# Who stores the diagonal blocks: ScalarE's queue instead of SyncE's, and a reordered first chunk

## The reference

```python
h = concatenate([meta_tokens, x])
proj = rms_norm(h) @ w_in          # q, k, v, z, two gates a and b per head, pool input, two output gates
qkv = silu(causal_depthwise_conv(qkv, 4 taps));  q, k = l2_normalize(q), l2_normalize(k)
o = chunk_gated_delta_rule(q, k, v, g, beta)       # 8 heads of 128
y = sigmoid(g_a) * (rms(o) * silu(z)) + sigmoid(g_b) * multiscale_causal_pool(pool_in)
h = h + y @ w_out
h = h + (silu(gate) * val) @ w_down                # from rms_norm(h) @ w_up, conv of 3 taps
out = rms_norm(h)[16:]

# inside chunk_gated_delta_rule, for each chunk and head:
lower = strict_lower((k * beta) @ k.T * decay)     # step KK
tinv  = inverse(lower + eye)                       # unit lower triangular
u, w  = tinv @ (v * beta), tinv @ (k * beta * exp(g))
v_new = u - w @ state;  o_i = q @ state + qk @ v_new
state = state * g_tot + k.T @ v_new                # carried from chunk to chunk
```

## Time and profile before

| what | value |
|---|---|
| median of 3 executions | 1813.52 us (1812.1 to 1817.27) |
| profiled execution | 1815.34 us, its span 1813.5 us |
| mean granted TensorE clock | 0.974 |
| TensorE busy | 1703.6 us, 94% of the span |
| VectorE, ScalarE, GpSimd busy | 899.9, 609.6, 479.9 us |
| transfers | 167.41 MB, 92 GB/s over the span |
| SyncE's queue, ScalarE's queue | 130.39 MB, 36.28 MB |

### The profile page before, as it was taken

The page is one execution under the profiler, slowest core; times in us unless marked ns, Lnnn a source line. Parts: engine busy times, 40 slices in busy tenths (PEclk is TensorE's granted clock), DMA queues, the critical chain, the costliest instruction groups (busy, mean ns, idle before and its releaser), DMA issues.

```text
span 1813.5 us, 30705 instructions
## 1 busy us (share of the span) xinstructions
PE 1703.6 (94%) x12131; PEld 1626.9 (90%) x12131; DVE 899.9 (50%) x971; ACT 609.6 (34%) x984; POOL 479.9 (26%) x469
## 2 busy tenths in 40 slices
PE   6999999975989998998969989999999999999997
PEld 6999999975989988898869989989989989989986
DVE  5565544573435444344352365455455455456457
ACT  6334474432424343343332442212212212212213
POOL 3222222152443344424402122122222222222220
PEclk9999999987999999999989999999999999999999
DMA  5223433335353635454395101111111111111112
GB/s 184 82 90 111 130 122 98 97 105 162 105 137 108 159 93 140 102 142 116 87 289 184 34 26 58 35 57 47 35 58 46 35 58 46 35 58 46 36 45 93
DMA packets 239653, 167.41 MB, mean 92 GB/s; under 512 B 43880, under 2 KB 225991, under 8 KB 238456
## 3 DMA queue, kind: packets, MB, share of 16 engines
q1 hardware_dynamic: 205492, 130.39, 25.4%
q10 hardware_dynamic: 33892, 36.28, 6.2%
q0 software_dynamic: 224, 0.12, 0.0%
HBM read 124.40 MB, written 42.37 MB: 92 GB/s over the span
## 4 chain that ended last, share of the span: by engine, by line
PE 86%; DVE 6%; DMA 3%; issue 3%; ACT 2%; DVEq 0%; ACTq 0%; SPq 0%; POOL 0%; POOLq 0%
PE gb L786 61%; PE db L1114 14%; PE db L925 5%; DMA yb_d<-ybs 1%; PE db L839 1%; DMA yo<-ot_d 1%; PE db L990 1%; PE db L991 1%; DVE cacc L1585 1%; DVE vb L1749 1%; DVE hx L1876 1%; PE db L1067 1%; PE db L922 0%; ACT hx L1160 0%; DVE h L1869 0%
## 5 line engine op out<-in xcount | busy, mean ns | idle before, releaser
L786 PE MATMUL gb<-u_hi,w_hi 128*128 128x342 f32 (+2 forms) x2520 | 827.2, 328 | 14.7 <-ACT ht L1457 5.7
L786 PE MATMUL gb<-u_lo,w_hi 128*128 128x342 f32 (+2 forms) x2520 | 813.3, 323 | 0.0
L786 PE MATMUL gb<-u_hi,w_lo 128*128 128x342 f32 (+2 forms) x2520 | 810.2, 322 | 0.0
L672 POOL TENSOR_TENSOR w_lo<-w_raw,w_hi 128x1024 fp32r<-128x1024 f32 x128 | 323.9, 2534 | 1114.6 <-ACT w_hi L1156 1114.6
L786 PEld LDWEIGHTS gb<-u_hi,w_hi 128*128 128x128 f32 x2520 | 481.4, 191 | 19.1 <-issue 15.9
L786 PEld LDWEIGHTS gb<-u_lo,w_hi 128*128 128x128 f32 x2520 | 481.6, 191 | 0.4
L786 PEld LDWEIGHTS gb<-u_hi,w_lo 128*128 128x128 f32 x2520 | 480.3, 191 | 0.0
L1948 DVE TENSOR_TENSOR h<-h,db 128x512 f32<-128x512 f32 x176 | 117.6, 685 | 59.4 <-PE db L1114 58.7
L1114 PE MATMUL db<-w_hi,a_hi 128*128 128x512 f32 x352 | 140.7, 400 | 2.9 <-DVE a_lo L1972 2.9
L1114 PE MATMUL db<-w_lo,a_hi 128*128 128x512 f32 x352 | 139.7, 397 | 0.0
L1114 PE MATMUL db<-w_hi,a_lo 128*128 128x512 f32 x352 | 139.7, 397 | 0.0
(11 more groups left out here) (234 smaller groups left out, 1725.9 us busy)
## 6 DMA issues: line engine op xcount, KB each, us to landing
w_raw<-in_w_in SPq DMA_DIRECT2D x53, 512.0 KB, 4.1
w_raw<-in_w_up SPq DMA_DIRECT2D x44, 512.0 KB, 3.8
w_raw<-in_w_down SPq DMA_DIRECT2D x22, 512.0 KB, 3.4
qkT_d<-sl ACTq DMA_DIRECT2D x16, 576.0 KB, 2.8
kv_d<-tm ACTq DMA_DIRECT2D x16, 576.0 KB, 3.4
tk<-kv_d SPq DMA_DIRECT2D x9, 1024.0 KB, 5.1
kT<-qkT_d SPq DMA_DIRECT2D x9, 512.0 KB, 4.8
qT<-qkT_d SPq DMA_DIRECT2D x9, 512.0 KB, 7.2
```

What stands on the lines that cost most here:

```text
L672: pool.tensor_tensor(w_lo[:, n % SLOTS, :], w_raw[:, n % SLOTS, :], w_hi[:, n % SLOTS, :].bitcast(F32), ALU.subtract).then_inc(s_wlo, 1)
L786: mm = pe.matmul(gb[:, bank, 0:w], wt, u, start=(k == 0 and m == 0), stop=(k == KT - 1 and m == 2))
```

## The change

Three things. The four stores of `blocks_out` move from SyncE's stream to ScalarE's: ScalarE does them in its step KK (and after the projection of the fourth pool group for chunk 0), with the wait for `s_ev["KK"]`. SyncE keeps the wait for their landing and the loads of `blk`, and does these at the head of a turn, ahead of the three weights. In the first chunk, the last pool group's projection comes before KK(0), QK(0) comes behind pool tile 0, VectorE does the KK company behind the third window instead of the second, `kT` for chunk 1 is loaded before `grow` and `tk`, `qT` behind the blocks, and ScalarE's `decays(1)` stands behind pool tile 5.

```diff
--- before.py
+++ after.py
@@ -130,7 +130,7 @@
 
 
 
-FIRST_PLAN = [("pool", j) for j in range(5)] + ["QK"] + [("pool", j) for j in range(5, KT)]
+FIRST_PLAN = [("pool", 0), "QK"] + [("pool", j) for j in range(1, KT)]
 
 
 
@@ -286,6 +286,10 @@
         def square(p):
 
             return slice(SQ * p, SQ * (p + 1))
+
+        def by_rows(m):
+
+            return m.rearrange("(h p) c -> p h c", h=HEADS)
 
         def over_heads(m, n=HEADS):
             return m.unsqueeze(1).broadcast_to([P, n, P])
@@ -492,9 +496,6 @@
                 sp.dma_start(dst[:, :, :], rows_d[bass.ds(c * HEADS, HEADS), r, :].unsqueeze(0).broadcast_to([P, HEADS, P])
                              ).then_inc(done, 16)
 
-            def by_rows(m):
-                return m.rearrange("(h p) c -> p h c", h=HEADS)
-
             def sub_blocks(m, e):
 
                 return m.rearrange("(g e r) (f c) -> e f g r c", e=2, r=SUB, f=2)[e][e]
@@ -505,9 +506,6 @@
 
             def blocks_out(c):
 
-                sp.wait_ge(s_ev["KK"], 2 * c + 2)
-                for p in range(P // SQ):
-                    sp.dma_start(by_rows(blk_d)[square(p)], at_m[square(p), :, square(p)]).then_inc(s_bst, 16)
                 sp.wait_ge(s_bst, 16 * (P // SQ) * (c + 1))
                 for e in range(2):
                     sp.dma_start(sub_rows(blk, e), sub_blocks(blk_d, e)).then_inc(s_blk, 16)
@@ -538,22 +536,21 @@
             load_row(brow, 1, 1, s_br)
             sp.wait_ge(s_sz, 16)
             blocks_out(0)
+            sp.wait_ge(s_ps["QK"], 2)
+            load_kT(1)
             sp.wait_ge(s_kg, 1)
             sp.wait_ge(s_qd, 1)
             load_row(grow, 0, 1, s_gr)
             sp.wait_ge(s_plo, 4)
             load_tk(0)
-            sp.wait_ge(s_ps["QK"], 2)
-            load_kT(1)
+            blocks_back(0)
             load_qT(1)
-            blocks_back(0)
             sp.wait_ge(s_gfree, U_ZG)
             sp.wait_ge(s_yb[0], 16 * 4)
             sp.wait_ge(s_yb[1], 16 * 4)
             sp.dma_start(yl[:, :], yb_d[0:P, :]).then_inc(s_yl, 16)
 
             def chunk_loads(n, last):
-                blocks_out(n)
                 sp.wait_ge(s_vb, n)
                 sp.wait_ge(s_kd, n)
                 load_tk(n)
@@ -568,11 +565,13 @@
                     load_qT(n + 1)
 
             with sp.Fori(0, HEADS - 1) as i:
+                blocks_out(i + 1)
                 for j, c0 in enumerate((Z_COL, GA_COL, GB_COL)):
                     load_w(W_ZG + 3 + j, cols(w_in, c0 + P + P * i), i)
                 chunk_loads(i + 1, False)
                 sp.wait_ge(s_gg, i + 1)
                 sp.dma_start(yl[:, :], yb_d[bass.ds(P + P * i, P), :]).then_inc(s_yl, 16)
+            blocks_out(NCH - 1)
             for n in range(3):
                 load_w(W_OUT + n, cols(w_out, n * P))
             chunk_loads(NCH - 1, True)
@@ -1002,8 +1001,8 @@
                 return [n for n in among if STEPS.index(n) % 2 == STEPS.index(name) % 2]
 
             pe.wait_ge(s_tm, QKV_TILES)
+            project(W_POOL + 3, U_POOL + 9)
             step("KK", 0, None)
-            project(W_POOL + 3, U_POOL + 9)
             for name in FIRST_PLAN:
                 if name[0] == "pool":
                     project_pool(name[1])
@@ -1314,6 +1313,12 @@
                 act.activation(ex[:, :, :], ex[:, :, :], ACT.Exp).then_inc(s_dec, 1)
                 act.activation(grow[:, :, :], grow[:, :, :], ACT.Exp).then_inc(s_eg, 1)
 
+            def blocks_out(c):
+
+                act.wait_ge(s_ev["KK"], 2 * c + 2)
+                for p in range(P // SQ):
+                    act.dma_start(by_rows(blk_d)[square(p)], at_m[square(p), :, square(p)]).then_inc(s_bst, 16)
+
             for g, group in enumerate(GROUPS):
                 if g < 3:
                     act.wait_ge(s_g, 3 * (W_POOL + g))
@@ -1338,6 +1343,8 @@
                     act.wait_ge(s_g, 3 * (W_POOL + 3))
                     w_high(W_ZG)
                     decays(0)
+                if g == 3:
+                    blocks_out(0)
                 act.wait_ge(s_pw, g + 1)
                 act.activation(p_hi[:, group, :], pool_out(group)[:, 16:], ACT.Copy).then_inc(s_phi, 1)
             act.wait_ge(s_g, U_WPOOL)
@@ -1364,7 +1371,9 @@
                     act.activation(heads(dst, h), dbank(name, h), ACT.Copy).then_inc(s_ev[name], 1)
 
             def act_step(name, c, last=False):
-                if name == "Y1" and not last:
+                if name == "KK":
+                    blocks_out(c)
+                elif name == "Y1" and not last:
                     decays(c + 1)
                 elif name == "Y0":
                     act.wait_ge(s_ps["V"], 2 * c)
@@ -1393,7 +1402,8 @@
             for name in FIRST_PLAN:
                 if name[0] == "pool":
                     scale_pool(name[1])
-            decays(1)
+                    if name[1] == 5:
+                        decays(1)
 
             def gates(u, i):
 
@@ -1774,6 +1784,7 @@
                 elif q == 1:
                     key_rows(0)
                     decays(0)
+                elif q == 2:
                     dve_step("KK", 0)
                     decayed_keys(0)
                     decayed_queries(0)
```

## The result

The changed kernel takes 1783.78 us (median of 4 executions, 1780.32 to 1788.88) against 1812.81 us before on the same chip, ratio 0.9838 with a 95% interval of 0.9808 to 0.9868: 29 us faster. I had forecast 1771, range 1764 to 1783. The direction was right, and so was what removes the stall; almost 13 us are missing. The profiled execution took 1780.32 us, its span 1778.5, which is the fast end of the four.

A forecast was written before the change was run, and what follows sets the result against it. TensorE, 86% of the chain, was held at X0 by the diagonal blocks' trip through DRAM and GpSimd. Loop 39.1 plus first chunk 3 gave 42.1 us off the profiled 1815.34; the median forecast was 1771 us, range 1764 to 1783.

The forecast's parts named there:

- The stall at X0 and its tail: TensorE's 28.4 us of waits at the inverse's first product, and slow-clock matmuls behind them, would go; turns take 52.92 us.
- The trip of the blocks: From at_m through DRAM and GpSimd to bds: loads leave sooner, making X0's input ready 2.0 us (0.4 to 3.3) early.
- `sol` leg: The 3.91 us from the sol stores to the bds load, counted unchanged but with its own chance to shrink.
- The rule on issuing engines: Transfers from several engines share 16 DMA engines, so a second queue saves at most issue time; order alone gives the same sum.
- The 1.2 us that I gave for the issue time: By the rule on issuing engines, the most the second queue brings; the stall's cover does not need it.
- The sum "7 x 52.92": Loop: seven periods of 408.0 us become seven stall-free turns, 37.6 us less; with turn 7's 1.5 us tail, 39.1 us.
- The first chunk: Moving QK(0) and kT out of the chain of pool stores gains 3 us, at most 4.4 from the two together.
- (a): Rival: part of the X0 stall stays, half of the loop's gain is lost, 1791 us; chance 8%.
- (c): Rival: slower, because issuing the four stores holds ScalarE; 1841 us at 4 us each; chance 3%.
- My signs of being wrong: X0 still waits over 2 us in most turns, TensorE newly waits at O or a weight, or first P1 comes later.

The follow-up runs named there:

- mask late: The changed kernel with GpSimd's mask(i + 2) moved behind state_parts(i + 1) instead of ahead of it: 1770.29 us, ratio 0.9746.
- the kernel with one input from PSUM: The changed kernel with VectorE's output_scale writing the reciprocal and factor into PSUM bank mb, GpSimd's order untouched: 1768.58 us, ratio 0.9761.
- the order alone: The changed kernel with the four block stores back in SyncE's queue, still ahead of the three weights: 1782.92 us, ratio 0.9815.
- the queue alone: The changed kernel with SyncE's three weights again ahead of the loads of blk, the stores staying on ScalarE: 1779.33 us, ratio 0.9794.
- the undo of KK(0) and the windows: The changed kernel with mask behind state_parts, plus KK(0) back ahead of the last pool projection and VectorE's KK company behind the second window: 1772.15 us, ratio 0.978.
- the first chunk alone: The changed kernel with the loop as before the change, stores on SyncE behind the weights, keeping only the first chunk's new order: 1806.06 us, ratio 0.9938.

## Why the prediction was wrong, step by step

- **The stall at X0 and its tail: right.** The wait went whole and the clock behind X0 is granted in full. A turn without them is 52.9 us, as mask late and the kernel with one input from PSUM show to 0.1 us.
- **The trip of the blocks: right.** Issue 2.02 us (forecast 1.83 to 3.06), loads of `blk` 4.9 us after `at_m` (3.1 to 6.0), the `sol` leg shorter as I had left open. X0's input is ready 4.6 us ahead of its use, more than the 2.0 I had counted.
- **The rule on issuing engines: right that the queue isn't needed.** But "the order alone" was only half of it: the queue alone is enough as well. The 1.2 us that I gave for the issue time is only the difference between two issues of four stores, 3.06 and 1.83 us; nothing in the sum rests on it.
- **The sum "7 x 52.92": the step that failed.** It took a turn without the stall to be a turn without any wait. I listed what the moved steps cost on SyncE and ScalarE, and never asked where GpSimd would now be. Its substitution ends 21.4 us after `at_m`, 28.3 before, so `mask` no longer queues behind it but is released by QK's eviction, together with VectorE's output scale. In the profile that is 1.7 us on the product in each of six turns (the last has no `mask`) and 17.4 - 7.6 = 9.8 us on TensorE's waits at OT. The seven periods from X0 at 474.37 to X0 at 855.98 take 381.6 us: one of 56.05 with the slow stretch, five of 54.5 to 54.6, and the last, without `mask`, 52.8. 7 x 52.92 is 370.4. That is 11.2 us lost, of 408.0 - 370.4 = 37.6 expected; in mask late the seven take 370.0. The profiled executions of the changed kernel and of mask late are 11.8 us apart, the medians 13.5. Mask late's median, 1770.3, is where I had put the change, but that is in part luck: it also has 2.4 us in the first chunk and the first turn's wait at OT that my sum did not have.
- **The first chunk: right in sign, too small.** Forecast 3 us, measured 5.4 over twelve profiles. I had priced the reorder of KK(0) as a risk only; the first store leaves 2.2 us sooner with the new order, which is about what is missing; of these, the undo of KK(0) and the windows gave back 1.2 in its one profile.
- **The rivals: none of them.** (a) came nearest, with a part of the gain lost: it had 1791, and what was lost was 13 us and not 20, by another mechanism. (c) looked at ScalarE for the new wait; it was on VectorE. My signs of being wrong named a new wait at O or at a weight, not at OT. The range of 1764 to 1783 held no case in which another engine, now early, gets in the way.

What stays open: how the first chunk's 5.4 us split between KK(0), QK(0) and `kT`, why the times give the first chunk alone 11 us and its share beside the loop's part 4.4, and why the changed kernel scatters over 8.6 us in its executions and mask late over 2.2.

## What to carry to other kernels

When a stall is taken away, follow every engine that gets early by it, not only those that get more to do: an engine that was late met nobody, and on time it meets its neighbour. Look for it in the turn where that engine is early already: here the first turn of before showed the meeting. In these traces a VectorE product of two SBUF tensors that started behind a GpSimd instruction on SBUF tensors waited out the rest of it, whatever its own size (1.86 us for 0.17), so look in the profile for a tiny product with the duration of a large GpSimd one. The cures are cheap: order GpSimd's work behind the next wait (1770.3 us in place of 1783.8), put one small operand in PSUM (1768.6), or issue the one-input work of VectorE first (6.3 us more).

## What the runs showed of the hardware that I had not expected

- The wait goes both ways, and the lead is small: `mask` 0.05 us ahead makes VectorE's small product 1.87 us, VectorE's large product 0.05 us ahead makes `mask` 2.93.
- Two GpSimd instructions straight behind each other let no two-input product in between (in the first turn of the changed kernel `kgt`, 1.22 us elsewhere, starts at 438.15 and takes 4.85, while GpSimd makes two low parts from 437.22, 4.69 us together); two with a drain between do.
